# Feed-forward layers that project tokens neither divided nor centred: mean and norm are applied to the products

## The reference, cut to what matters

```python
def layer_norm(x, g, b):
    mu = jnp.mean(x32, axis=-1, keepdims=True)
    var = jnp.mean(jnp.square(x32 - mu), axis=-1, keepdims=True)
    y = (x32 - mu) * lax.rsqrt(var + LN_EPS)
    return y * g + b

def swiglu(x, w_in, w_out):
    h = x @ w_in
    return (jax.nn.silu(h[..., :D_FF]) * h[..., D_FF:]) @ w_out

x = layer_norm(ALPHA * x + mix, ln_mix_g[layer], ln_mix_b[layer])
x = layer_norm(ALPHA * x + swiglu(x, ffn_w_in[layer], ffn_w_out[layer]), ...)
```

## Time and profile before

| | us |
|---|---|
| median of 3 runs (1223.03 to 1224.64) | 1223.81 |
| the profiled execution | 1226.05 |
| its span from first to last instruction | 1224.1 |
| PE busy in it (matmuls) | 1185.0 |
| DVE busy | 860.9 |
| ACT busy | 615.9 |
| POOL busy | 147.1 |

### The profile page before, as it was taken

How to read it: one execution, slowest core, us unless ns; L and a number is a source line. 1 busy time by engine, 2 the same in 40 slices (tenths; PEclk the granted TensorE clock), 3 DMA queues, 4 the chain that set the end, 5 groups by cost and what they waited for, 6 DMA issues and landing times.

```text
span 1224.1 us, 22938 instructions
## 1 busy us (share of the span) xinstructions
PE 1185.0 (97%) x9272; PEld 1103.1 (90%) x9272; DVE 860.9 (70%) x1443; ACT 615.9 (50%) x1002; POOL 147.1 (12%) x115
## 2 busy tenths in 40 slices
PE   6999999999999999999999899999989999999996
PEld 3777888888888999999999899999989998999996
DVE  5795884468789767656498687674479967866644
ACT  4432654467564455652453544453466765445433
POOL 0000000000000000003001313210007930222000
PEclk8999999999999999999999999999999999999999
DMA  9856412333222356442544345455433233545540
GB/s 386 346 196 257 157 69 70 113 128 138 103 104 104 138 179 217 170 138 70 180 175 161 139 174 205 172 189 189 173 107 135 104 115 128 199 178 181 197 172 35
DMA packets 28900, 195.59 MB, mean 160 GB/s; under 512 B 3464, under 2 KB 3728, under 8 KB 6416
## 3 DMA queue, kind: packets, MB, share of 16 engines
q1 hardware_dynamic: 27776, 191.90, 43.6%
q10 hardware_dynamic: 1040, 2.50, 0.6%
HBM read 193.33 MB, written 1.05 MB: 159 GB/s over the span
## 4 chain that ended last, share of the span: by engine, by line
PE 86%; DVE 5%; ACT 4%; DMA 2%; issue 1%; POOL 1%; SPq 0%; ACTq 0%; DVEq 0%
PE ps L489 25%; PE ps L490 24%; PE ps L491 24%; PE ps L840 2%; PE ps L514 2%; DMA ada_room<-in_weights 1%; PE ps L532 1%; DVE w_lo L1757 1%; PE ps L827 1%; PE ps L660 1%; DVE w_lo L1760 1%; DMA ring<-in_weights 1%; ACT x_hi L1455 1%; PE ps L1065 1%; PE ps L719 1%
## 5 line engine op out<-in xcount | busy, mean ns | idle before, releaser
L1151 ACT ACTIVATE w_hi<-ring 128x1024 fp32r<-128x1024 f32 x284 | 294.9, 1056 | 290.8 <-PE ps L491 202.5
L1760 DVE TENSOR_TENSOR w_lo<-ring,w_hi 128x1024 fp32r<-128x1024 f32 x266 | 327.7, 1251 | 154.5 <-ACT w_hi L1151 147.7
L489 PE MATMUL ps<-x_hi,w_hi 128*128 128x258 f32 (+1 forms) x1216 | 347.4, 286 | 7.6 <-DVE x_lo L2140 4.1
L490 PE MATMUL ps<-x_lo,w_hi 128*128 128x258 f32 (+1 forms) x1216 | 344.8, 284 | 0.0
L491 PE MATMUL ps<-x_hi,w_lo 128*128 128x258 f32 (+1 forms) x1216 | 344.4, 283 | 0.0
L489 PEld LDWEIGHTS ps<-x_hi,w_hi 128*128 128x128 f32 x1216 | 231.7, 191 | 11.6 <-issue 11.4
L490 PEld LDWEIGHTS ps<-x_lo,w_hi 128*128 128x128 f32 x1216 | 232.1, 191 | 0.1
L491 PEld LDWEIGHTS ps<-x_hi,w_lo 128*128 128x128 f32 x1216 | 231.6, 190 | 0.0
L489 PE MATMUL ps<-g_hi,w_hi 128*128 128x256 f32 x608 | 171.2, 282 | 4.8 <-ACT logit L1570 1.5
L490 PE MATMUL ps<-g_lo,w_hi 128*128 128x256 f32 x608 | 170.3, 280 | 0.0
L491 PE MATMUL ps<-g_hi,w_lo 128*128 128x256 f32 x608 | 170.3, 280 | 0.0
(11 more groups left out here) (377 smaller groups left out, 1942.2 us busy)
## 6 DMA issues: line engine op xcount, KB each, us to landing
ring<-in_weights SPq DMA_DIRECT2D x148, 1024.0 KB, 4.8
o_sb<-in_weights SPq DMA_DIRECT2D x10, 1024.0 KB, 7.2
ada_room<-in_weights SPq DMA_DIRECT2D x10, 1024.0 KB, 8.6
ring<-in_weights SPq DMA_DIRECT2D x8, 512.0 KB, 4.2
ring<-in_weights SPq DMA_DIRECT2D x8, 448.0 KB
V<-in_weights SPq DMA_DIRECT2D x3, 1024.0 KB, 24.8
dft<-in_dft ACTq DMA_DIRECT2D x1, 1026.0 KB, 7.4
X<-in_x SPq DMA_DIRECT2D x1, 1024.0 KB, 5.0
```

The source lines that it names most:

```text
L489: mm(dst, w_h, x_h, start=start, stop=False, skip_group_check=True)
L490: mm(dst, w_h, x_l, start=False, stop=False, skip_group_check=True)
L1151: do(w_hi[:, q % 2, part], ring[:, q % RING, part], ACT.Copy).then_inc(S("hi_ready"), 1)
L1760: v.tensor_tensor(w_lo[:, q % 2, part], ring[:, q % RING, part], w_hi[:, q % 2, part], ALU.subtract).then_inc(S("lo_ready"), 1)
```

## The change

- `ffi0` and `ffi1` project X times g as it is, not centred. In `raw_norm` DVE now interleaves terms and `x_lo` as for the norms without a mean; ACT rounds `x_hi` straight after each term.
- PE sums X at k = 4 of slot 0 and folds at k = 6, sums the squares at k = 4 of slot 1 and folds at k = 6.
- DVE centres X afterwards, in two instructions of 128x1024, and only for the squares and the residual; ACT squares in two instructions of 128x1024, behind `hi` of slot 1's second half.
- The two extra columns are now g and b. Column 256 of a product is g times the weights; the DVE computes once `mean_part` = -mean x rstd, and in every unit adds `mean_part` x column 256 to each of the two products (two more instructions of 128x256), with two more waits on its own semaphores. Silu waits for the first of them, `gated` also for the second.
- Slot 3 waits for that first correction of unit 0 (bank 3 holds the mean) in place of `norm_root`.
- The shift copy takes two columns per bank. Two semaphores of the kernel's start are merged into others that exist.

```diff
+        mean_part = sq[:, 4, :]
+        def gain_and_shift(l):
+            return vcol(f"mix_g{l}", 0, 2 * KD).rearrange("p (o k) -> p k o", o=2)
...
             def raw_project(n, name, norm, moved, before=0, last_slot=None, cols=SEQ + 2):
+                centred = NORMS[norm][1]
...
-                        if fixed and t == 1:
+                        if fixed and t == 1 and not centred:
                             grouped_sum(sq, S("norm_squares"), since("squares", norm), 1)
                         if fixed and t == 3:
-                            pe.wait_ge(S("norm_root"), since("root", norm) + 1)
+                            if centred:
+                                pe.wait_ge(S("raw_scaled"), N_FIN + before + 1)
+                            else:
+                                pe.wait_ge(S("norm_root"), since("root", norm) + 1)
...
                         if fixed and t == 0:
                             pe.wait_ge(S("norm_split"), since("split", norm) + k + 1)
-                        if fixed and t == 1 and k == 2:
+                        if fixed and t == 0 and centred and k == 4:
+                            grouped_sum(X, S("norm_in"), since("in", norm), 0)
+                        if fixed and t == 0 and centred and k == 6:
+                            fold_groups(norm, 0, raw_mean, S("norm_mean"))
+                        if fixed and t == 1 and centred and k == 4:
+                            grouped_sum(sq, S("norm_squares"), since("squares", norm), 1)
+                        if fixed and t == 1 and k == (6 if centred else 2):
                             fold_groups(norm, 1, raw_var, S("norm_var"))
...
             def feed_forward(l):
-                centring(f"mix{l}")
...
             def split_raw(name, stage, gain):
                 centred = NORMS[name][1]
+                for k in range(KD):
+                    act.wait_ge(S("norm_in"), since("in", name) + k + 1)
+                    do(x_hi[:, k, :], X[:, k, :], ACT.Copy, scale=gain(k)).then_inc(S("norm_hi"), 1)
+                    if not centred:
+                        do(sq[:, k, :], X[:, k, :], ACT.Square).then_inc(S("norm_squares"), 1)
                 if centred:
-                    hi(STARTS[stage] + 1, halves=(1,))
                     act.wait_ge(S("norm_part"), since("part", name) + 1)
                     do(gate[:, 0, :], ps[:, 2, 0:SEQ], ACT.Copy).then_inc(S("norm_part_moved"), 1)
...
+                hi(STARTS[stage] + 1, halves=(1,))
+                for k in range(0, KD if centred else 0, KD // 2):
+                    act.wait_ge(S("norm_centred"), since("centred", name) + k + KD // 2)
+                    do(sq[:, k:k + KD // 2, :], X[:, k:k + KD // 2, :], ACT.Square).then_inc(S("norm_squares"), KD // 2)
...
-                    if m and not centred:
+                    if m:
                         split(m - 1)
+                split(KD - 1)
+                lo(STARTS[after[stage]] + 1, halves=(0,))
                 if centred:
-                    lo(STARTS[after[stage]] + 1, halves=(0,))
                     dve.wait_ge(S("norm_in"), since("in", name) + KD)
                     dve.wait_ge(S("norm_mean"), since("mean", name) + 1)
-                    for k in range(KD):
-                        v.tensor_tensor(X[:, k, :], X[:, k, :], raw_mean, ALU.subtract)\
-                            .then_inc(S("norm_centred"), 1)
-                        if k:
-                            split(k - 1)
-                split(KD - 1)
-                lo(STARTS[after[stage]] + 1, halves=(1,) if centred else (0, 1))
+                    dve.wait_ge(S("norm_split"), since("split", name) + KD)
+                    for k in range(0, KD, KD // 2):
+                        a = X[:, k:k + KD // 2, :]
+                        v.tensor_tensor(a, a, wide(raw_mean, KD // 2), ALU.subtract)\
+                            .then_inc(S("norm_centred"), KD // 2)
+                lo(STARTS[after[stage]] + 1, halves=(1,))
...
                     raw_shift(u, bank)
-                    raw_product(product[u % 2], bank).then_inc(S("raw_scaled"), 1)
+                    if fixed and t == 0:
+                        chain.step(v.scalar_tensor_tensor(mean_part, raw_mean, -1.0, rstd[:, 0:SEQ],
+                                                          ALU.mult, ALU.mult))
+                    raw_product(product[u % 2], bank).then_inc(S("products"), 1)
+                    if fixed and t == 0:
+                        chain.join()
+                    dve.wait_ge(S("products"), t + (N_FFI * l + 1))
+                    for b in range(2):
+                        a = product[u % 2][:, b, :]
+                        last = v.scalar_tensor_tensor(a, mean_part, shift_of[:, u, b, 0:1], a, ALU.mult, ALU.add)
+                        if b == 0:
+                            last.then_inc(S("raw_scaled"), 1)
+                    last.then_inc(S("values_scaled"), 1)
                     dve.wait_ge(S("gate_ready"), t + (N_FFI * l + 1))
+                    dve.wait_ge(S("values_scaled"), t + (N_FFI * l + 1))
```

More of the change, by code:

```diff
@@ L570, in fold_sums @@
                 pe.wait_ge(S("sums_moved"), 1)
-                mm(ps[:, 6, :], ones[:, :], V[:, HC, :], start=True, stop=True).then_inc(S("meansq_0"), 1)
+                mm(ps[:, 6, :], ones[:, :], V[:, HC, :], start=True, stop=True).then_inc(S("sums_done"), 1)
             def first_tile(t, k):
@@ L1203, in _ @@
             rounded_half(0, 0)
-            act.wait_ge(S("meansq_0"), 1)
-            do(rstd[:, :], ps[:, 6, :], ACT.Sqrt, bias=eps[:, 0:1], scale=1.0 / 32).then_inc(S("root_0"), 1)
+            act.wait_ge(S("sums_done"), 2)
+            do(rstd[:, :], ps[:, 6, :], ACT.Sqrt, bias=eps[:, 0:1], scale=1.0 / 32).then_inc(S("sums_moved"), 1)
             for p in range(ADA_PAIRS):
@@ L1407, in _, with round_shift @@
             round_y(HEADS - 1)
-            def round_shift(bias):
-                do(x_both[0][:, :, SEQ:], bias.rearrange("p (k o) -> p k o", o=1).to_broadcast([P, KD, 2]),
-                   ACT.Copy).then_inc(S("shift_hi"), 1)
+            def round_shift(columns):
+                do(x_both[0][:, :, SEQ:], columns, ACT.Copy).then_inc(S("shift_hi"), 1)
             for t in range(N_OZ + 2, N_OZ + N_MOUT - 1):
@@ L1415, in _ @@
             act.wait_ge(S("y_ready"), HEADS)
-            round_shift(modl[:, 3 * KD:4 * KD, 0])
+            round_shift(in_twos(modl[:, 3 * KD:4 * KD, 0]))
             load_root()
@@ L1517, in _ @@
             units(N_EVIN, "evin", evin_root)
-            round_shift(vcol("mix_b0", 0, KD))
+            round_shift(gain_and_shift(0))
             units(N_EVOUT, "evout")
@@ L1531, in gating @@
                         act.wait_ge(S("ffi_moved"), t + (N_FFI * l - 1))
-                    do(gate[:, u % 2, :], product[u % 2][:, 0, :], ACT.Silu, bias=shift_of[:, u, 0:1])\
+                    do(gate[:, u % 2, :], product[u % 2][:, 0, :], ACT.Silu, bias=shift_of[:, u, 0, 1:2])\
                         .then_inc(S("gate_ready"), 1)
@@ L1543, in _ @@
             feed_forward(0)
-            round_shift(vcol("mix_b1", 0, KD))
+            round_shift(gain_and_shift(1))
             def move_odin(t):
@@ L1813, in _ @@
             rest_of_half(0)
-            dve.wait_ge(S("root_0"), 1)
+            dve.wait_ge(S("sums_moved"), 2)
             chain.step(v.reciprocal(rstd[:, :], rstd[:, :]))
@@ L2155, in residual, with rest_of_shift @@
                 dve.wait_ge(S("norm_in"), since("in", name) + KD)
-            def rest_of_shift(n, bias):
+            def rest_of_shift(n, columns):
                 dve.wait_ge(S("shift_hi"), n + 1)
-                v.tensor_tensor(x_both[1][:, :, SEQ:], bias.rearrange("p (k o) -> p k o", o=1)
-                                .to_broadcast([P, KD, 2]), x_both[0][:, :, SEQ:], ALU.subtract)
+                v.tensor_tensor(x_both[1][:, :, SEQ:], columns, x_both[0][:, :, SEQ:], ALU.subtract)
             def raw_norm(name, stage, index, term, gain):
@@ L2235, in _ @@
                         last = v.scalar_tensor_tensor(g_lo[:, 2 * t + b, :], product[t % 2][:, b, :],
-                                                      shift_of[:, t % 4, b:b + 1], g_hi[:, 2 * t + b, :],
+                                                      shift_of[:, t % 4, b, 1:2], g_hi[:, 2 * t + b, :],
                                                       ALU.add, ALU.subtract)
@@ L2382, in gating @@
                     raw_shift(u, bank)
-                    raw_product(product[u % 2], bank).then_inc(S("raw_scaled"), 1)
+                    if fixed and t == 0:
[11 more added lines that the diff above has]
+                    last.then_inc(S("values_scaled"), 1)
                     dve.wait_ge(S("gate_ready"), t + (N_FFI * l + 1))
+                    dve.wait_ge(S("values_scaled"), t + (N_FFI * l + 1))
                     if not fixed or t >= 4:
                         dve.wait_ge(S("ffi_split"), t + (N_FFI * l - 3))
```

(2 more changed lines are left out.)

29 lines of the change are left out of this document (10 added, 19 removed).

## The result

The changed kernel takes 1235.68 us (median of 5 runs, 1233.49 to 1236.46) against 1223.81: the ratio is 1.0086, 95% interval 1.0073 to 1.0100. It is slower, as forecast, and by 4 to 5 us more than forecast (1230.4): inside the range of 1221.5 to 1236.5, above the forecast's own range of 1226.5 to 1234. The profiled execution took 1233.49 (span 1231.7).

A forecast was written before the change was run, and what follows sets the result against it. PE, busy 97%, bounds the kernel; DVE matters only where PE waits for it. Waits of 14.3 less gains of 7.75 give net +6.6: median 1223.8 to 1230.4 us, range 1221.5 to 1236.5, forecast's own 1226.5 to 1234.

The forecast's parts named there:

- the heads: Starts of ffi0 and ffi1: the new order shortens them, gains 4.7 and 3.05, together 7.75 us.
- slots 3 to 6: Early slots of each feed-forward: PE waits for w_lo, about 3.5 us in all per stage.
- the loop: Units 4 to 15: a unit takes DVE 5.8 against PE's 5.74, about 0.1 us a stage; DVE stays just in time.
- slot 21: Late in each feed-forward: PE waits 3.55 us for unit 19's `gated`; lower bound 2.1.
- rival "clock": The pause at slot 21 lowers PE's clock, costing 1.6 us in each stage, +3.2: 1233.6; chance 0.12.
- Head of ffi0: Border from evout into slot 0: PE goes on without a pause, low clock gone; slot 0 takes 7.3, gain 4.7 us.
- Head of ffi1: Border into ffi1: PE pauses 1.6 because `hi`, waiting for DMA, stands ahead of x_hi; gain 3.05 us.
- Unit 0, later by 3.8: First unit: later squares' sum, mean_part and correction move w_lo of slot 3 to 12.75 behind slot 0; PE waits 1.0.
- Units 1 to 3: DVE takes 0.52 more in each, 19.7 against PE's 17.2: 2.5 us of PE waits, 3.5 with slot 3.
- drained lag: Rival: DVE wins back enough by unit 19, so slot 21 does not wait: 1223.1 us; chance 0.14.
- Faster: Rival: unit 0's lead and DVE's idle time in units 1 to 3 cover the added work; only gains stay: 1216.1; chance 0.18.

The follow-up runs named there:

- run 7: Changed kernel with POOL's g_lo held until DVE has finished the next pair of w_lo: 1221.23 us, ratio 0.9974.
- Run 5: Changed kernel with ACT's `hi` of slot 2 ahead of its move of the squares' sum: 1232.27 us, ratio 1.0060.
- run 4: Changed kernel with X's scalings on DVE and shifts on ACT moved into the projection behind: 1228.33 us, ratio 1.0033.
- Run 8: Kernel before, old head, with corrections by a zero mean_part and POOL's g_lo held until the next w_lo pair is done: 1223.48 us, ratio 1.0000.
- run 10: Three kernels on the changed one: first, edits of run 1, run 4, run 5, run 6, 1218.20 us; plus run 7, 1216.07; only run 5, run 6, run 7, 1217.27.
- run 6: Changed kernel with ACT's `hi` of slot 1 in the second feed-forward moved behind the x_hi and the sum's move: 1233.42 us, ratio 1.0067.
- Run 3: Kernel before, old head, with the corrections added to every unit by a mean_part of zero: 1236.84 us, ratio 1.0095.
- run 1: Changed kernel with unit 19 reordered on DVE: product and corrections first, `gated` between the halves of slot 21's w_lo: 1228.66 us, ratio 1.0037.

## Why the prediction was right, and where it fell short

**The account.** In the two profiled executions the heads gave 6.3 (forecast 7.75); slots 3 to 6 cost 7.1 (7.0), the loop 0.3 (0.2), slot 21 6.6 (7.1) and the lower clock behind it 3.2 (in the sum: nothing). That is some 10.8, and the two stretches grew by 10.6. So the cause was named rightly: DVE's unit uses up its lead and PE waits at slots 3 to 6 and 21. The branch that came is the rival "clock" (1233.6), not the forecast; that the time stayed under the top of the range, by 0.8, is in part luck, as the heads' shortfall of 1.4 was in no branch.

**Head of ffi0, 4.7 forecast, 4.2 measured.** No pause and clock 1.00, as said. Slot 0 took 7.7, not 7.3; half of the difference is the sum, whose step to the next matmul is 1.21 against 1.00 in slot 1. The sum starts at 686.62 and the eighth term ends at 687.22, so its last matmuls may have waited for that term; no run tests this. I had given the terms no wait.

**Head of ffi1, 3.05 forecast, 2.1 measured.** The reason held (the first x_hi behind an `hi` that waits for the DMA; PE's pause 1.76, forecast 1.6); the sum then took 0.4 more than in slot 1. The later runs that keep this head put the pause at 1.3 to 2.9, as the load happened to come: I had priced it from one execution.

**Unit 0, later by 3.8.** w_lo of slot 3 was to start 12.75 behind slot 0, at 704.08; it started at 703.97. mean_part took 0.41 (taken: 0.44). The wait at slot 3 was 0.86 for 1.0, but 1.40 in ffi1, where g_lo was first; with g_lo held (run 7) it is 0.87 in both. Run 5 confirms the step: with `hi` earlier the wait is gone in ffi0 and 0.32 in ffi1.

**Units 1 to 3, 3.5 with slot 3; measured 3.5 in both stages.** The two corrections and the wait between product and correction took 0.92 and the wait for silu fell from 0.58 to 0.18: 0.52 a unit, as forecast. From w_lo of slot 3 to w_lo of slot 6 passed 723.71 - 703.97 = 19.7. The waits alone, 3.0, would hide this: each restart costs 0.1 more.

**Loop, 5.8 forecast, 5.70 measured.** The wait between product and correction cost only 0.04 there; that between gated and g_hi is 0.14. (The bounds of the added waits, 0.04 and 0.25, give 5.63 to 5.84, not to the 5.9 of the prediction.) DVE was just in time all the same: at 5.70 it wins back some 0.5 in twelve units, and the next ones, behind ACT's shifts, are 6.41 and then 5.87 long. Slot 21 waited 3.10 and 3.48 for 3.55. Without the shifts, and without the scalings, it waited 2.05 and 2.72 (run 4). The Trainium skill, page "VectorE: DVE Perf Modes", section "The DRAIN you can't avoid", whose rule gives 5.63, came a little nearer to the unit than I did. The trace agrees at the added wait (0.04) and not at gated (0.14), and slot 21 did not wait 1.5 less.

**The clock, forecast as a rival at 0.12: it came, twice.** This is the step that was mis-sized: I added the clock's 1.6 to no term, and it was 1.6 in each stage with the restart, 3.2 of the 4.0 us by which the forecast fell short in the profiled executions. The weaker heads took another 1.4, and slot 21 gave 0.5 back. I had compared 3.55 with pauses of 4.1 and 1.7 and found it nearer to 4.1; the forecast should have followed that sentence. The Trainium skill, page "TensorE: Matmul & The Clock Gate", section "HAM oscillation — how this bites in real kernels", warned that long enough idle gaps halve the clock; the trace agrees behind the idle times of 2.94 and 3.32.

**What I took as given and should have asked.** The prediction says that a w_lo pair is "long (2.90 for two, where two alone take 2.35)" and prices the unit with 2.90. It never asks what makes it long. Had it looked at POOL's row at the same time, it would have seen the change's size in another light: the unit held 0.55 us that were not its own, about as much as the change added to it (5.11 to 5.70). Run 8 shows that this was the whole cost of the corrections. The later unit 0 keeps a cost of its own: with g_lo held the changed kernel still loses 1.7 a stage (run 7).

The rival "drained lag" described the kernel with that one wait on POOL, not the changed kernel: there slot 21 does not wait (run 7). "Faster" is what the three kernels of run 10 show.

## What to carry to other kernels

When an operation has two durations in one trace, look at what the other engines do during the long one before adding work to its engine: here two subtracts with all operands in SBUF, a pair on DVE and one on POOL, held each other up by 0.55 and 0.84 us, and a wait on the idle engine repaired a change that had made the kernel slower. An edit that loads an engine is priced by its lead over the bound, and a lead can be spent once: two edits that are each covered need not be covered together. Where a wait is forecast at 3 us for TensorE, put the clock behind it into the sum. Read a loss as the distance over several slots and not as the sum of the waits alone, which left out 0.5 of 3.5 here.

## What was not expected of the hardware

**DVE and POOL.** w_lo (two inputs and the output in SBUF) takes 1.23 a half alone, g_lo 0.74. Where they meet, only the one that starts second is longer: g_lo up to 1.81, its end 0.57 to 0.61 behind that of the half ahead of it, or w_lo up to 1.80 a half. X's scalings (two inputs in SBUF as well) are held up too, 1.76 for three against 1.27. Beside the product (one input in PSUM) neither is longer, 0.74 and 0.68. The corrections overlap g_lo by some 0.2 us only in run 7 and take 0.90 against 0.88; what a full overlap would cost them was not tried.

**The clock and the pause.** The length of the pause alone does not say whether the clock falls. Three kernels had a wait of 2.94 at slot 21 of ffi0: the changed one fell (0.51), run 6 fell, run 5 did not. Windows behind the pause, run 5, then run 6:
```profile
814.00:816.00 2.00, 1.87 (x15) 1.90 (x16) 1.05 (x2) 2.00 (x3) 0.73 (x1) 1.00 1.00 422
```
```profile
816.00:818.00 2.00, 1.85 (x10) 1.88 (x11) 1.03 (x3) 2.00 (x3) 0.73 (x1) 0.63 0.98 414
```
Run 3's 2.90 was followed by 1.00 as well (its windows above). In run 4 it fell behind 2.56 in ffi1 and behind 2.86 at the head, and not behind 1.89:
```profile
812.00:814.00 2.00, 2.00 (x17) 2.00 (x18) 1.86 (x3) 1.13 (x2) 1.73 (x1) 1.00 0.92 385
1013.00:1015.00 2.00, 2.00 (x12) 2.00 (x10) 2.00 (x6) 1.35 (x4) 0.00 (x0) 0.50 0.00 0
1143.00:1145.00 2.00, 2.00 (x11) 2.00 (x10) 1.96 (x5) 0.00 (x0) 0.00 (x0) 0.50 0.00 0
```
No single pause up to 1.9, with PE busy up to it and from it on, was followed by the lower level in these runs. What the lower level cost varied too: inside the two stages and at their heads it lasted 13 to 27 matmuls, 1.2 to 2.6 us.

**Two paces of the projection behind.** A slot of ffo (matmuls of 256 columns) took 5.63 in some executions and 5.70 in others, at granted clock 1.00 and with nothing waiting: the same code in the kernel before and in run 1, windows of 60 us in ffo0:
```profile
820.00:880.00 60.00, 60.00 (x514) 60.00 (x513) 29.16 (x26) 24.20 (x24) 1.10 (x2) 1.00 0.53 189
```
```profile
820.00:880.00 60.00, 60.00 (x508) 60.00 (x507) 30.39 (x30) 25.01 (x26) 1.47 (x2) 1.00 0.54 193
```
It is worth 0.7 us a stage (62.67 for 61.95), and came in both stages of run 1, in the first of run 4 and in the second of the first kernel of run 10. The slots of 258 columns stayed at 5.745 everywhere. What decides the pace was not tried.
